# First attention of a transformer kernel: sums of the softmax from a ones column in V, and products on the two 64-row halves of the array, two heads at a time

## The chip, the cores and the metric

The program runs on one core of a Trainium2 chip. One launch computes two blocks of a small transformer. The time is the device time of one launch in microseconds (us). Five engines run their own instruction streams and meet at semaphores: PE (TensorE, products), DVE (VectorE), ACT (ScalarE), POOL (GpSimd) and SP, which issues most of the DMAs.

## The reference, cut to what matters

256 tokens, width 1024, 16 heads of 64. Everything is fp32. The stage that changes is the forgetting attention of the first block:

```python
def forgetting_attention(q, k, v, logf_cum):
    seq = q.shape[1]
    scale = HEAD_DIM ** -0.5
    qf = q.astype(jnp.float32)
    kf = k.astype(jnp.float32)
    outs = []
    for blk in range(seq // Q_BLOCK):
        q0 = blk * Q_BLOCK
        q1 = q0 + Q_BLOCK
        s = jnp.einsum("bqhd,bkhd->bhqk", qf[:, q0:q1], kf[:, :q1]) * scale
        s = s + logf_cum[:, :, q0:q1, None] - logf_cum[:, :, None, :q1]
        mask = (q0 + jnp.arange(Q_BLOCK))[:, None] >= jnp.arange(q1)[None, :]
        s = jnp.where(mask, s, -jnp.inf)
        p = jax.nn.softmax(s, axis=-1).astype(v.dtype)
        outs.append(jnp.einsum("bhqk,bkhd->bqhd", p, v[:, :q1]))
    return jnp.concatenate(outs, axis=1)
...
            o = forgetting_attention(q, k, v, logf_cum).reshape(bsz, seq, D_MODEL)
            x = x + o @ w_o[b_i]
```

`logf_cum` is the running sum of the forget gates' logarithms, one row per head. The term of the query is constant along a softmax row and falls out of it, so the kernel adds only the term of the key. Before it come the projections to K, V and Q, after it the product with `w_o`, then a router and eight experts, then the second block. All of these stay as they are, except for the order of the first of the four `w_o` tiles.

## The kernel before, in words

All order is written out by hand: each engine has one list of instructions, and semaphores join them. PSUM has eight banks. `bank(n)` is use n of banks 0 to 3, taken round robin (`turn`); PE may write a bank again when whoever read its last use has counted up `taken`. `lbank(n)` is use n of banks 4 to 7 (`lend`, `lent_back`) in the same manner. Weights come as tiles of 128 x 2048: SP loads a tile into `ring`, ACT rounds it to `w_hi` (`feed`, L1000), DVE makes the rest `w_lo` (`feed_lo`, L1655), and a product of weights is three products, high by high, high by low and low by high (L2555 to L2557).

The attention works on 32 units. Unit i is head i // 2 and query block i % 2; a unit has k_len = 128 keys for block 0 and 256 for block 1. `attend_step` gives for each unit, on PE: the score product (L2799) of `q_pad` with `kT`, an fp32 product, of which every one stands as two rows (two passes) in the trace; `kT` holds two heads on its 128 rows, so `q_pad` comes in two copies, each with the other head's 64 rows zero. Then, into the same bank, the forget sums in two fp32r products, high part `c_hi` (L2804) and low part `c_lo` (L2805), each by a broadcast column of an identity that picks the head's row; and the causal mask (L2806). DVE takes the negative row maximum (L1948). ACT takes the exponential and its row sum (L1087; the sum is a second instruction). DVE takes the reciprocal of the sum (L1954) and multiplies the probabilities by it (L1955). PE turns the probabilities in blocks of 128 x 128 (L2814), ACT copies them out of PSUM (L1093), and PE multiplies `v_tok`, both heads of a pair wide and stationary, by them (L2826, fp32, two passes). The result has features on the partitions. Scores run ahead: the turn of unit i comes LAG = 3 units after its scores and the product with V two more later. Of each result 64 rows count, and ACT and DVE split them into high and low (L1047, L1051; L1936, L1940), upper and lower half apart, since the next product needs both as its moving part. Three weight tiles of `w_o` are made by DVE inside the stage, after units 5, 10 and 15. Four groups of two products of `w_o` follow (`project`), and the first waits until the last pair of heads is split.

Of the kernel before, what the change touches and what calls it, by code (L numbers as in the profile page):

```python
# [13 lines left out]
P = 128  # L14
# [41 lines left out]
V_LAG = 2  # L56
FIRST_CONSTS = 5
# [3 lines left out]
def build(nc, a):  # L61

    with ExitStack() as ctx:
# [90 lines left out]
        q_pad = [region(4096, DC, T), region(10240, DC, T)]  # L154
        kT = region(6144, DC, T)
        v_tok = region(8192, TT, D)
# [4 lines left out]
        c_hi = act_hi[:, 0, 0:T]  # L161
        c_lo = act_lo[:, 0, 0:T]
# [117 lines left out]
        half_logs = tab(544, 2 * TT * LH)  # L280
        top_i = sb("top_i", [P, TT, 8], U32)
# [74 lines left out]
        def attention_order(units):  # L356

            s, w = {}, {}
            for i in range(units + LAG):
                if i < units:  # L360
                    s[i] = turn(1)
                if i >= LAG:
                    w[i - LAG] = turn(1)
            return s, w

        AT1 = attention_order(2 * NH)
# [133 lines left out]
        A_O1 = lend(8)  # L500
# [123 lines left out]
        heads_done = sem("heads_done")  # L624
        consts = sem("consts")
# [31 lines left out]
        q_padded = sem("q_padded")  # L657
# [207 lines left out]
        def _(pool):  # L865
# [49 lines left out]
            pool.memset(q_pad[0], 0.0)  # L915
            pool.memset(q_pad[1], 0.0).then_inc(q_padded, 1)
            pool.wait_ge(summed, PAIRS)
            pool.memset(c_hi.bitcast(F32), 0.0)
            pool.memset(c_lo.bitcast(F32), 0.0).then_inc(c_padded, 1)
# [40 lines left out]
        def _(eng):  # L960
# [120 lines left out]
            def attend_step(i, order, units, causal, base, sc=sc, pT=pT):  # L1081

                s_use, w_use = order
                if i < units:
                    eng.wait_ge(sc_ready, base + i + 1)
                    k_len = P * (i % 2 + 1) if causal else T
                    give(eng.activation(sc[:, i % 4, 0:k_len], bank(s_use[i])[:, 0:k_len], ACT.Exp,  # L1087
                                        bias=nmax[:, i % 4, :], accum_out=esum[:, i % 4, :]), s_use[i])
                if LAG <= i < units + LAG:
                    j = i - LAG  # L1090
                    k_len = P * (j % 2 + 1) if causal else T
                    eng.wait_ge(done, w_use[j] + 1)
                    give(eng.activation(pT[:, j % pT.shape[1], 0:k_len], bank(w_use[j])[:, 0:k_len], ACT.Copy), w_use[j])  # L1093

            def attend(order, units, causal, base, a_o, h_o, dst_at):

                left = list(range(units // 4))
                for i in range(units + LAG):
                    attend_step(i, order, units, causal, base)
# [2359 lines left out]
```

## Time and profile before

| | us |
|---|---|
| median of three runs | 2083.45 |
| lowest and highest | 2080.48, 2083.79 |
| the profiled execution | 2080.59 |
| its span | 2078.8 |
| from the first score product to the first product of `w_o` | 446.69 to 491.91, that is 45.22 |

The span runs from the first to the last instruction, and 1.8 us lie around it. PE is busy for 96% of it. A matmul's row ends by a model, so the start of the next row tells more than the length of one: where n rows of a kind stand together, the step between starts is (whole length less one row's length) divided by n - 1. Rows named PEld are loads of the stationary part. Times are from the start of the span; a bracket gives the idle time of the engine before the instruction and what ended it.

### The profile page before, as it was taken

How to read it: one execution, taken by the hardware profiler on the slowest of the kernel's cores; microseconds unless marked ns; L12 is line 12 of the kernel's file. 1: busy time of each engine (PE TensorE's matmuls, PEld its weight loads, DVE VectorE, ACT ScalarE, POOL GpSimd, SP SyncE). 2: the span in 40 equal slices, each digit the busy share in tenths (PEclk: the TensorE clock that was granted, in tenths of full speed). 3: DMA queues.
4: the chain of work that ended last, by engine and by line, in shares of the span. 5: the costliest groups of instructions: out<-in, count | busy, mean ns of one | idle time of the engine just before them, and what ended most of it. 6: DMA issues, size and time to landing. Idle time of an engine off the chain costs nothing.

```text
span 2078.8 us, 32665 instructions
## 1 busy us (share of the span) xinstructions
PE 1994.7 (96%) x13049; PEld 1782.3 (86%) x13049; DVE 1510.1 (73%) x1745; ACT 1246.6 (60%) x1477; POOL 38.8 (2%) x69
## 2 busy tenths in 40 slices
PE   8999999989799999999999999899899999999998
PEld 8988899989688888787888888799899998998997
DVE  6966777665688888888888988866656555756554
ACT  5674443555577777777777776746345445775443
POOL 2000000000000000000000000000000000000000
PEclk9999999999899999999999999989999999999999
DMA  8314555532599999989898989635014554424552
GB/s 251 103 44 153 188 182 184 164 120 102 179 359 336 379 340 337 382 326 394 325 394 325 394 323 395 215 99 172 23 41 150 196 184 141 143 99 146 191 186 98
DMA packets 265219, 455.44 MB, mean 219 GB/s; under 512 B 10545, under 2 KB 147226, under 8 KB 265114
## 3 DMA queue, kind: packets, MB, share of 16 engines
q1 hardware_dynamic: 263304, 448.37, 61.6%
q0 software_dynamic: 1424, 5.24, 0.6%
q8 instruction: 78, 1.28, 0.3%
q10 hardware_dynamic: 386, 0.32, 0.0%
q14 instruction: 27, 0.22, 0.0%
HBM read 451.81 MB, written 2.10 MB: 218 GB/s over the span
## 4 chain that ended last, share of the span: by engine, by line
PE 81%; DVE 8%; ACT 5%; issue 3%; DMA 2%; SPq 1%; DVEq 0%; ACTq 0%
PE bank L2555 22%; PE bank L2556 21%; PE bank L2557 21%; PE bank L2743 3%; PE bank L2693 2%; DVE w_lo L1655 2%; DVE w_lo L2069 2%; PE bank L2745 2%; DMA ring<-in_moe_w_up 1%; ACT w_hi L1303 1%; ACT w_hi L1000 1%; PE bank L2959 1%; PE bank L2583 1%; PE bank L2799 1%; PE bank L2826 1%
## 5 line engine op out<-in xcount | busy, mean ns | idle before, releaser
L1655 DVE TENSOR_TENSOR w_lo<-ring,w_hi 128x2048 fp32r<-128x2048 f32 x160 | 365.5, 2292 | 196.7 <-ACT w_hi L1000 196.4
L2555 PE MATMUL bank<-w_hi,a_both 128*128 128x512 f32 (+1 forms) x1040 | 372.5, 358 | 14.8 <-DVE w_lo L2069 11.5
L2555 PE MATMUL bank<-a_both,w_hi 128*128 128x256 f32 x1248 | 360.1, 289 | 10.9 <-DVE a_both L1692 3.9
L2557 PE MATMUL bank<-w_hi,a_both 128*128 128x512 f32 (+1 forms) x1040 | 363.5, 350 | 0.0
L2556 PE MATMUL bank<-w_lo,a_both 128*128 128x512 f32 (+1 forms) x1040 | 363.5, 350 | 0.0
L2069 DVE TENSOR_TENSOR w_lo<-ring,w_hi 128x2048 fp32r<-128x2048 f32 x144 | 327.7, 2290 | 47.8 <-ACT w_hi L1303 47.8
L1000 ACT ACTIVATE w_hi<-ring 128x2048 fp32r<-128x2048 f32 x160 | 304.6, 1908 | 92.7 <-PE bank L2557 86.4
L2556 PE MATMUL bank<-a_both,w_hi 128*128 128x256 f32 x1248 | 355.3, 285 | 0.0
L2557 PE MATMUL bank<-a_both,w_lo 128*128 128x256 f32 x1248 | 355.2, 285 | 0.0
L1303 ACT ACTIVATE w_hi<-ring 128x2048 fp32r<-128x2048 f32 x144 | 276.1, 1919 | 95.5 <-PE bank L2557 84.3
L2069 DVE TENSOR_TENSOR w_lo<-work,w_hi 128x2048 fp32r<-128x2048 f32 x120 | 274.7, 2289 | 21.0 <-ACT w_hi L1303 19.6
L1303 ACT ACTIVATE w_hi<-work 128x2048 fp32r<-128x2048 f32 x120 | 230.5, 1921 | 91.3 <-PE bank L2557 86.4
L2555 PEld LDWEIGHTS bank<-a_both,w_hi 128*128 128x128 f32 x1248 | 241.6, 194 | 15.6 <-issue 9.6
L2556 PEld LDWEIGHTS bank<-a_both,w_hi 128*128 128x128 f32 x1248 | 241.7, 194 | 1.4
L2555 PEld LDWEIGHTS bank<-w_hi,a_both 128*128 128x128 f32 x1040 | 197.3, 190 | 52.6 <-DVE w_lo L2069 25.2
L2557 PEld LDWEIGHTS bank<-a_both,w_lo 128*128 128x128 f32 x1248 | 241.6, 194 | 0.0
L2555 PE MATMUL bank<-w_hi,act_hi 128*128 128x512 f32 x608 | 240.7, 396 | 0.0
L2556 PE MATMUL bank<-w_lo,act_hi 128*128 128x512 f32 x608 | 237.1, 390 | 0.0
L2557 PE MATMUL bank<-w_hi,act_lo 128*128 128x512 f32 x608 | 237.1, 390 | 0.0
L2557 PEld LDWEIGHTS bank<-w_hi,a_both 128*128 128x128 f32 x1040 | 197.2, 190 | 26.4
L2556 PEld LDWEIGHTS bank<-w_lo,a_both 128*128 128x128 f32 x1040 | 197.4, 190 | 23.5
L2555 PEld LDWEIGHTS bank<-w_hi,act_hi 128*128 128x128 f32 x608 | 114.2, 188 | 27.1 <-issue 4.8
(462 smaller groups left out, 2756.1 us busy)
## 6 DMA issues: line engine op xcount, KB each, us to landing
ring<-in_moe_w_up SPq DMA_DIRECT2D x72, 1024.0 KB, 8.2
work<-in_moe_w_gate SPq DMA_DIRECT2D x72, 1024.0 KB, 9.0
ring<-in_moe_w_down SPq DMA_DIRECT2D x56, 1024.0 KB, 6.8
work<-in_moe_w_down SPq DMA_DIRECT2D x32, 1024.0 KB, 7.3
ring<-in_w_up SPq DMA_DIRECT2D x32, 1024.0 KB, 5.5
ring<-in_w_down SPq DMA_DIRECT2D x32, 1024.0 KB, 4.9
ring<-in_moe_w_gate SPq DMA_DIRECT2D x16, 1024.0 KB, 5.1
work<-in_moe_w_up SPq DMA_DIRECT2D x16, 1024.0 KB, 7.5
```

What stands on the lines that cost most here:

```text
L1000: return eng.activation(w_hi[:, slot, :], ring[:, slot, :], ACT.Copy)
L1303: eng.activation(w_hi[:, slot, :], raw_tile(j), ACT.Copy).then_inc(m_hi, 1)
L1655: V.tensor_tensor(w_lo[:, i % SLOTS, :], ring[:, i % SLOTS, :], w_hi[:, i % SLOTS, :].bitcast(F32), ALU.subtract).then_inc(lo_made, 1)
L2069: V.tensor_tensor(w_lo[:, slot, :], raw_tile(j), w_hi[:, slot, :].bitcast(F32), ALU.subtract).then_inc(m_lo, 1)
L2555: PE.matmul(out, left[0], right[0], start=start, stop=False, **kw)
L2556: PE.matmul(out, left[0], right[1], start=False, stop=False, **kw)
L2557: return PE.matmul(out, left[1], right[0], start=False, stop=stop, **kw)
L2583: mm = PE.matmul(bank(n)[:, 0:T], ones[:, :], sq[:, c, :], start=(c == 0), stop=(c == DC - 1))
L2693: mm = PE.matmul(out[:, 0:T], diag[:, i % DIAGS, :], glu[:, c, k:k + T], start=(i == first), stop=(i == DIAG_ENDS[g]))
L2743: PE.matmul(bank(n + i)[:, :].rearrange("p (k t) -> p k t", k=2), w_of[0], a_both[:, :, c, :], start=(c == 0), stop=False, skip_group_chec ...
L2745: mm = PE.matmul(bank(n + i)[:, 0:T], w_of[1], a_hi[:, c, :], start=False, stop=(c == DC - 1), skip_group_check=True)
L2799: mm = PE.matmul(out[:, 0:k_len], q_of(hh)[:, P * j:P * j + P], k_of(hh)[:, 0:k_len], start=True, stop=not causal)
```

## The change

Query, key and cumulative sums:

- `q_pad` becomes `q_sb`, one copy without zeros. The scores of two heads of a pair are two products of 64 rows, head 0 on rows 0 to 63 and head 1 on rows 64 to 127 of the array, into two banks.
- `c_hi` and `c_lo` become one tile `c_two`: rows 0 to 15 hold the high and rows 32 to 47 the low part, and the same again from row 64. `pass_two` is a column pattern with a one in both places, so a single fp32r product of 64 rows adds high and low. ACT and DVE each write one part more, and DVE makes `pass_two` with two small additions.
- V has a 65th column of ones for each head. The row sum is no longer taken by ACT nor applied to the probabilities: the turned probabilities are now stationary and V moves, 65 columns at a time, so the result has tokens on the partitions and the sums in a column. DVE takes the reciprocal for four (head, block) results and multiplies them in one instruction into `o_sb`. PE turns `o_sb` back to features (`turn_heads`), ACT and DVE split the turned bank over all 128 rows.

Order: step m has the two heads of pair m // 2 at query block m % 2. PE's step is scores of m, turns of m - 1, product with V of m - 2, and at odd m from 5 on the turning back of pair (m - 5) // 2. The first `w_o` tile goes by chunks, both banks in turn, each chunk waiting for its pair of heads; the last pair is turned back between chunks 3 and 4. The memory attentions of the second block keep their way, with the parameter for causal calls taken out.

PE, in the middle of the attention, before (units of 256 and 128 keys in turn; bank4 takes the product with V):

```order
L2799 MATMUL bank3<-work 128x256 [waits taken3]
L2804 MATMUL bank3<-act_hi 128x256
L2805 MATMUL bank3<-act_lo,act_hi 128x256
L2806 MATMUL bank3<-act_hi 128x128
L2814 MATMUL bank0<-ident,work 128x128 [waits prob_ready,taken0]
L2826 MATMUL bank4<-work 128x128 [waits taken0]
L2799 MATMUL bank1<-work 128x128 [waits taken1]
L2804 MATMUL bank1<-act_hi 128x128
L2805 MATMUL bank1<-act_lo,act_hi 128x128
L2806 MATMUL bank1<-act_hi 128x128
```

and PE there after the change, one step of 256 keys and the head of the next (L2860 scores, L2863 forget sums, L2865 mask, L2871 turns, L2881 V):

```order
L2860 MATMUL bank3<-work 128x256
L2863 MATMUL bank2<-act_hi,act_lo 128x256
L2863 MATMUL bank3<-act_hi,act_lo 128x256
L2865 MATMUL bank2<-act_hi 128x128
L2865 MATMUL bank3<-act_hi 128x128
L2871 MATMUL bank0<-ident,work 128x128 [waits taken2,taken0]
L2871 MATMUL bank1<-ident,work 128x128 [waits taken3,taken1]
L2881 MATMUL bank4<-work 128x65 [waits taken0]
L2881 MATMUL bank4<-work 128x65
L2881 MATMUL bank4<-work 128x65 [waits taken1]
L2881 MATMUL bank4<-work 128x65
L2860 MATMUL bank2<-work 128x128 [waits taken3,taken2]
```

Scores now use banks 2 and 3 at every step and turned probabilities banks 0 and 1, where before the two kinds took all four in turn.

DVE in the same stretch, before:

```order
L1948 TENSOR_REDUCE small<-bank3 128x1 [waits done]
L1954 RECIPROCAL small<-small 128x1 [waits taken1]
L1955 TENSOR_SCALAR work<-work,small 128x128 [waits vq]
L1948 TENSOR_REDUCE small<-bank1 128x1 [waits done]
L1954 RECIPROCAL small<-small 128x1 [waits taken3]
L1955 TENSOR_SCALAR work<-work,small 128x256 [waits vq]
L1936 TENSOR_TENSOR a_both<-bank4,a_both 64x256 [waits in_hi]
```

and after (L1961 maxima, L1975 and L1976 the division by the sums, L1665 a weight tile, L1940 the split):

```order
L1961 TENSOR_REDUCE small<-bank2 128x1 [waits done]
L1961 TENSOR_REDUCE small<-bank3 128x1 [waits done]
L1975 RECIPROCAL small<-bank6 128x4 [waits heads_done]
L1976 TENSOR_TENSOR work<-bank6,small 128x256 [waits vq]
L1961 TENSOR_REDUCE small<-bank2 128x1 [waits done]
L1961 TENSOR_REDUCE small<-bank3 128x1 [waits done]
L1665 TENSOR_TENSOR w_lo<-ring,w_hi 128x2048 [waits hi_made]
L1940 TENSOR_TENSOR a_both<-bank5,a_both 128x256 [waits in_hi]
```

The reciprocal and the scaling of each unit are gone from between the maxima. The weight tile still stands between two maxima.

The core of the diff, in the order forget sums and bank uses, ACT's loop, DVE's query part, division and loop, PE's loop and first `w_o` tile:

```diff
-        q_pad = [region(4096, DC, T), region(10240, DC, T)]
+        q_sb = region(4064, DC, T)
-        v_tok = region(8192, TT, D)
+        v_tok = region(8160, TT * NH, HD + 1).rearrange("p (j h) e -> p j h e", j=TT)
-        c_hi = act_hi[:, 0, 0:T]
-        c_lo = act_lo[:, 0, 0:T]
+        c_two = act_hi[:, 0, 0:T]
+        pass_two = act_lo[:, 0, 0:NH]
...
-        AT1 = attention_order(2 * NH)
+        AT1 = {}, {}
+        for m in range(NH + 1):
+            for i in range(2 * m, 2 * m + 2):
+                if m < NH:
+                    AT1[0][i] = turn(1)
+            for i in range(2 * m - 2, 2 * m):
+                if m:
+                    AT1[1][i] = turn(1)
...
+            def attend_tokens(order):
+                for m in range(NH + 1):
+                    k_len = P * (m % 2 + 1)
+                    for i in range(2 * m, 2 * m + 2):
+                        if m < NH:
+                            eng.wait_ge(sc_ready, i + 1)
+                            give(eng.activation(sc[:, i % 4, 0:k_len], bank(s_use[i])[:, 0:k_len], ACT.Exp, bias=nmax[:, i % 4, :]), s_use[i])
+                    if m % 2 == 0 and m > TURN_LAG:
+                        turned_heads_hi((m - TURN_LAG - 1) // 2)
+                    k_len = P * ((m - 1) % 2 + 1)
+                    for i in range(2 * m - 2, 2 * m):
+                        if m:
+                            eng.wait_ge(done, w_use[i] + 1)
+                            give(eng.activation(pT[:, i % 4, 0:k_len], bank(w_use[i])[:, 0:k_len], ACT.Copy), w_use[i])
...
-                V.scalar_tensor_tensor(q_pad[0][0:64, i, :], bank(n)[0:64, 0:T], HD ** -0.5, rstd[0:64, :], ALU.mult, ALU.mult)
-                give(V.scalar_tensor_tensor(q_pad[1][64:P, i, :], bank(n)[64:P, 0:T], HD ** -0.5, rstd[64:P, :], ALU.mult, ALU.mult), n)
+                give(V.scalar_tensor_tensor(q_sb[:, i, :], bank(n)[:, 0:T], HD ** -0.5, rstd[:, :], ALU.mult, ALU.mult), n)
...
+            def heads_by_sums(c):
+                n = A_O1 + 2 * c
+                eng.wait_ge(heads_done, c + 1)
+                out = lbank(n)[:, 0:4 * (HD + 1)].rearrange("p (u e) -> p u e", u=4)
+                link(V.reciprocal(head_rec[:, c % 2, :], out[:, :, HD]))
+                give_lent(V.tensor_tensor(o_sb[:, c % 2, :].rearrange("p (u e) -> p u e", u=4), out[:, :, 0:HD],
+                                          head_rec[:, c % 2, :].rearrange("p (u o) -> p u o", o=1).to_broadcast([P, 4, HD]), ALU.mult), n)
...
+                for m in range(NH):
+                    for i in range(2 * m, 2 * m + 2):
+                        score_max(i, order, P * (m % 2 + 1))
+                    if m in (2, 5, 7):
+                        feed_lo(min(T_Q + (m + 1) // 3 + SLOTS + (m == 7), T_MOE - 1))
+                    if m % 2 == 0 and m >= 4:
+                        heads_by_sums(m // 2 - 2)
+                    if m % 2 == 1 and m >= TURN_LAG + 2:
+                        heads_back((m - TURN_LAG - 2) // 2)
...
+                        outs = [open_bank(s_use[2 * m + r]) for r in range(2)]
+                        for r, at in HALVES:
+                            PE.matmul(outs[r][:, 0:k_len], q_sb[at, c, P * j:P * j + P], kT[at, c, 0:k_len], start=True, stop=False)
+                        for r, at in HALVES:
+                            one = pass_two[at, 2 * c + r:2 * c + r + 1].to_broadcast([CK, P])
+                            PE.matmul(outs[r][:, 0:k_len], one, c_two[at, 0:k_len], start=False, stop=False)
+                        for r, at in HALVES:
+                            PE.matmul(outs[r][:, P * j:P * j + P], pass_on, causal_mask, start=False, stop=True).then_inc(done, 1)
...
+                                mm = PE.matmul(out[:, at:at + HD + 1], pT[:, t % 4, P * b:P * b + P], v_tok[:, b, 2 * c + r, :], start=(b == 0), stop=(b == j))
...
-            for t in range(4):
-                if t == 0:
-                    got_lent(eng, A_O1 + 6)
-                    got_lent(eng, A_O1 + 7)
+            outs = [open_bank(U_WO), open_bank(U_WO + 1)]
+            for c in range(DC):
+                if c == DC - 4:
+                    turn_heads(DC - 1)
+                got_lent(eng, A_O1 + 2 * c + 1)
+                for i in range(2):
+                    mm = product(outs[i][:, 0:T], [v[:, c, P * i:P * i + P] for v in w], a_part(c), c == 0, c == DC - 1)
+                    if c == DC - 1:
+                        mm.then_inc(done, 1)
+            for t in range(1, 4):
                 project(T_WO + t, U_WO + 2 * t)
```

## Rows read from the trace of the kernel before

**Rows 1.** The page: busy time and share of each engine; the group of weight tiles' low parts.

```profile
PE 1994.7 (96%) x13049; PEld 1782.3 (86%) x13049; DVE 1510.1 (73%) x1745; ACT 1246.6 (60%) x1477; POOL 38.8 (2%) x69
...
L1655 DVE TENSOR_TENSOR w_lo<-ring,w_hi 128x2048 fp32r<-128x2048 f32 x160 | 365.5, 2292 | 196.7 <-ACT w_hi L1000 196.4
```

**Rows 2.** Stretches: length, busy PE, PEld, DVE, ACT, POOL (instructions), granted clock, DMA.

```profile
446.70:472.20 25.50, 20.88 (x162) 19.49 (x163) 20.77 (x61) 15.60 (x58) 0.00 (x0) 1.00 0.29 90
472.20:486.00 13.80, 13.80 (x118) 13.47 (x116) 11.85 (x43) 10.66 (x45) 0.00 (x0) 1.00 0.17 65
```

**Rows 3.** The chain that ended last, in order of time: start, length, what.

```profile
474.53 0.43 PE bank L2799 x2
...
485.91 0.43 PE bank L2799 x2
```

**Rows 4.** Timeline of PE, late in the attention: start, length, engine, line, operation.

```profile
485.30 0.61 PE L2826 MATMUL bank<-work 128*128 128x128 f32 x4
...
486.30 0.28 PE L2805 MATMUL bank<-act_lo,act_hi 128*128 128x256 f32 x1
486.41 0.22 PE L2806 MATMUL bank<-act_hi 128*128 128x128 f32 x1
```

**Rows 5.** Timeline of all engines at the start of the attention.

```profile
446.05 0.43 DVE L1919 SCALAR_TENSOR_TENSOR work<-bank,rstd 64x256 f32<-64x256 f32 x1
...
446.69 0.46 PE L2799 MATMUL bank<-work 128*128 128x128 f32 x2 [1.10 <-DVE work L1919]
...
447.15 0.28 PE L2806 MATMUL bank<-act_hi 128*128 128x128 f32 x1
...
447.47 0.29 DVE L1948 TENSOR_REDUCE small<-bank 128x1 f32<-128x128 f32 x1 [0.99 <-PE bank L2806]
...
449.13 0.37 ACT L1087 ACTIVATE work<-bank,small 128x128 f32<-128x128 f32 x1
```

**Rows 6.** Timeline of ACT, one of three places where a weight tile on DVE delays it.

```profile
462.95 0.47 ACT L1087 ACTIVATE work<-bank,small 128x256 f32<-128x256 f32 x1 [2.12 <-DVE small L1948]
```

**Rows 7.** Groups of DVE and ACT by line and shape: count, busy us, mean ns, idle before.

```profile
L1948 DVE TENSOR_REDUCE small<-bank 128x1 f32<-128x256 f32 x32 | 13.5, 422 | 6.9 <-PE bank L2799 3.4 <-PE bank L2806 3.2
...
L1087 ACT ACTIVATE work<-bank,small 128x256 f32<-128x256 f32 x32 | 15.1, 473 | 32.1 <-DVE small L1948 32.0
...
L1093 ACT ACTIVATE work<-bank 128x256 f32<-128x256 f32 x24 | 9.0, 377 | 0.4 <-PE bank L2814 0.3
```

**Rows 8.** Timeline of PE in the second block: products of 64 rows among full ones.

```profile
1826.87 0.61 PE L2826 MATMUL bank<-work,mem_v 128*128 128x128 f32 x4
1827.41 0.71 PE L3345 MATMUL bank<-work 64*128 64x256 f32 x4
...
1828.17 0.59 PE L3345 MATMUL bank<-work 64*128 64x256 f32 x2
1828.61 0.38 PE L3346 MATMUL bank<-work 64*128 64x128 f32 x2
1828.92 0.38 PE L2555 MATMUL bank<-w_hi,a_both 128*128 128x256 f32 x1
```

**Rows 9.** Timeline of PE in the second block: fp32 products that move 64 columns, then 128.

```profile
1509.58 0.39 PE L3222 MATMUL bank<-work 128*128 128x64 f32 x2
...
1510.03 0.39 PE L3222 MATMUL bank<-work 128*128 128x64 f32 x2
1510.25 1.56 PE L3228 MATMUL bank<-work 128*128 128x128 f32 x12
```

**Rows 10.** Timeline of PE at the end of the attention: the first product of `w_o`.

```profile
491.91 0.35 PE L2555 MATMUL bank<-a_both,w_hi 128*128 128x256 f32 x1 [1.80 <-issue]
```

**Rows 11.** PE in the second block: two stretches (clock after the busy time), one timeline row.

```profile
1496.00:1498.00 2.00, 1.89 (x32) 0.87 0.00 0
1498.00:1500.00 2.00, 1.39 (x7) 0.50 0.03 8
...
1501.20 2.88 PE L3228 MATMUL bank<-work 128*128 128x128 f32 x12
```

More of the change, by code:

```diff
@@ L1079, in ffn, with attend_step @@
                         feed(tile_of[g - 1][-1] + SLOTS)
-            def attend_step(i, order, units, causal, base, sc=sc, pT=pT):
+            def attend_step(i, order, units, base, sc=sc, pT=pT):
                 s_use, w_use = order
@@ L1090, in attend_step, with turned_heads_hi @@
                     j = i - LAG
-                    k_len = P * (j % 2 + 1) if causal else T
                     eng.wait_ge(done, w_use[j] + 1)
[L1093 to L1099, printed above, removed]
-                    if 9 <= i < units and i % 4 == 1:
-                        split_upper(a_o + left[0], h_o + left[0], dst_at + left[0])
-                    if 9 <= i < units and i % 4 == 3:
-                        c = left.pop(0)
-                        split_lower(a_o + c, dst_at + c)
-                for c in left:
-                    split_pair(a_o + c, h_o + c, dst_at + c)
+                    give(eng.activation(pT[:, j % pT.shape[1], 0:T], bank(w_use[j])[:, 0:T], ACT.Copy), w_use[j])
+            def turned_heads_hi(c):
+                eng.wait_ge(heads_turned, c + 1)
+                eng.activation(a_hi[:, c, :], lbank(A_O1 + 2 * c + 1)[:, 0:T], ACT.Copy).then_inc(in_hi, 1)
+            def attend_tokens(order):
+                s_use, w_use = order
+                for m in range(NH + 1):
[11 more added lines that the diff above has]
+                            give(eng.activation(pT[:, i % 4, 0:k_len], bank(w_use[i])[:, 0:k_len], ACT.Copy), w_use[i])
+                for c in range((NH - TURN_LAG - 1) // 2 + 1, DC):
+                    turned_heads_hi(c)
             def scaled_hi(u, gain):
@@ new lines, in heads_back, with attend_tokens @@
+            def heads_back(c):
+                heads_lo(A_O1 + 2 * c + 1, I_WO, c)
+            def attend_tokens(order):
+                for m in range(NH):
[7 more added lines that the diff above has]
+                        heads_back((m - TURN_LAG - 2) // 2)
+                for c in range(DC - 2, DC):
+                    heads_by_sums(c)
+                    heads_back(c - 1)
+                heads_back(DC - 1)
@@ L2824, in attend_step, with turn_heads @@
                     got(eng, w_use[t])
-                    for b in range(blocks):
+                    for b in range(TT):
                         mm = PE.matmul(out[:, at:at + P], v_of(hh, b), pT[:, t % pT.shape[1], P * b:P * b + P],
-                                       start=(b == 0), stop=(b == blocks - 1))
+                                       start=(b == 0), stop=(b == TT - 1))
                     if t % 4 == 3:
                         mm.then_inc(heads_done, 1)
-            def attend(order, units, causal, base, a_o, q_of, k_of, v_of):
-                for i in range(units + LAG + V_LAG):
-                    attend_step(i, order, units, causal, base, a_o, q_of, k_of, v_of)
+            def turn_heads(c):
+                got_lent(eng, A_O1 + 2 * c)
+                out = open_lent(A_O1 + 2 * c + 1)
+                for j in range(TT):
+                    mm = PE.transpose(out[:, P * j:P * j + P], o_sb[:, c % 2, P * j:P * j + P], ident[:, :])
+                mm.then_inc(heads_turned, 1)
```

142 lines of the change are left out of this document (69 added, 73 removed).

## Prediction, made before the changed kernel had run

> **What bounds the kernel now.** The page comes first: PE is busy for 96% of the span [rows 1], so a change is worth what it takes from PE's path or from a wait of PE. I then cut the attention, 446.69 to 491.91 us, into stretches. Late in it, from 472.2 to 486.0, PE is busy without a gap, DVE for 11.85 and ACT for 10.66 of 13.80 us: PE bounds. Before, from 446.7 to 472.2, PE is busy for 20.88 of 25.50 us [rows 2], and the reasons are the start and three weight tiles of 2.29 us on DVE [rows 1], each of which keeps the maxima and so ACT waiting (2.12 us in one place [rows 6]). After the last scores PE works off the tail until 491.91 [rows 10]. The chain of waits shows the steady pace: the 256-key score products of two units ten units apart stand at 474.53 and 485.91 [rows 3], 11.38 us for five heads, 2.28 each or 4.55 for a pair.
>
> **Prices of PE.** All of these are starts, not lengths. A full fp32 pass with 128 columns comes every (0.61 - 0.27) / 3 = 0.113 us, and the fp32r forget product of 256 columns is followed after 0.11 by the mask [rows 4]. By these a pair of heads before costs: scores 4 x (0.22 + 0.113) = 1.33 (two passes of 256 columns take from 1828.17 to 1828.61 in [rows 8]), forget sums 8 x 0.115 = 0.92, mask 4 x 0.113 = 0.45, turns 6 and V 12 passes x 0.113 = 2.03: 4.73, against 4.55 measured, so the list holds to 4%.
>
> **Part by part, on PE, for a pair.**
> *Scores on halves.* The nearest rows are in the second block, where L3345 (256 columns) and L3346 (128) work on 64 rows, three heads in turn on halves 0, 1, 0 [rows 8]. The first four L3345 stand together, so the second head's passes began before the first head's narrower ones: the halves do overlap. Two heads took 1828.17 - 1827.41 = 0.76 us, where one alone took 0.75 to the next full product. So I take 0.50 for 256 keys and 0.25 for 128, against 0.88 and 0.45 if the halves ran one after the other.
> *Changing between 64 and 128 rows.* The last full pass begins at 1826.87 + 0.61 - 0.27 = 1827.21 and should be through at 1827.32; the half one starts at 1827.41. On the way back the last pass begins at 1828.72, is through at 1828.83, and the full one starts at 1828.92. So each change costs 0.09 us, and there are two in a step, 0.36 in a pair. The Trainium skill, "TensorEngine Tiling (Array Packing)", Key Properties, speaks against the change here: switching the tiling mode drains the engine. The rows agree that it costs something, and I go by their 0.09.
> *Forget sums.* Eight products become two concurrent pairs, 0.12 each, 0.24. No row shows fp32r on 64 rows; without overlap they cost 0.46.
> *Mask, turns.* The same numbers, 4 and 6, 1.13; turning back adds 2, 0.23.
> *V.* Still 12 passes, now with 65 columns instead of 128. Rows 9 have the price of that: from 1509.58 to 1510.03 four passes that move 64 columns, 0.112 each, and the same at 128 columns, (1.56 - 0.27) / 11 = 0.117. Half the columns save nothing, since each pass has its own load of 128 stationary columns. So 12 x 0.113 = 1.36. The Trainium skill, "TensorE: Matmul & The Clock Gate", Back-to-back issue gap, would have the step follow the moving columns down to about 60; by that V would cost about half. The rows say no.
> The sum for a pair is 0.75 + 0.36 + 0.24 + 1.13 + 0.23 + 1.36 = 4.07. By steps: odd m (256 keys: scores 0.50, sums 0.12, changes 0.18, mask 0.23, two turns 0.23, eight passes of V 0.90, turning back 0.23) 2.38; even m 1.68.
>
> **The loop that takes PE's place.** Scores always use banks 2 and 3, so the scores of step m + 1 wait for both exponentials of step m. At 256 keys: scores, sums and change 0.71 to the first mask product; 0.32 from there to DVE's start (447.15 to 447.47 [rows 5]); one maximum's step 0.34 and the second maximum 0.42; ACT 0.04 later for 0.47 [rows 7]; 0.05 back to PE: 2.35. At 128 keys with 0.29 and 0.37 [rows 5]: 0.46 + 0.32 + 0.20 + 0.29 + 0.04 + 0.37 + 0.05 = 1.73. A pair makes 4.08. PE and this loop are equal to within the reading, which leaves no slack, so I take 4.15 for a pair, 1.75 for a lone even step. DVE's own load is 1.4 of maxima, 0.2 + 0.42 for the division, 0.42 for the split, about 2.4; ACT's 2 x (0.47 + 0.37) of exponentials, 2 x 0.38 + 2 x 0.27 of copies and 0.38 for the split, 3.4: both below 4.15, and the copies end about when the next exponential is due.
>
> **Start, tiles, tail.**
> *Start.* The query part on DVE is one instruction of 0.43 instead of two, so the first scores come 0.43 earlier, at 446.26 [rows 5]. Steps 0 and 1 have free banks. The first exponential comes 2.44 after the first scores, as before (446.69 to 449.13); four exponentials, 2 x 0.27 and 2 x 0.38 apart, end 1.4 later, and step 2 starts at 3.9. Steps 2 to 14 are six pairs and one even step: 6 x 4.15 + 1.75 = 26.65.
> *Weight tiles.* They stand after the maxima of steps 2, 5 and 7. A tile of 2.29 begins 1.25 (even) or 1.75 (odd) into the step; the next maximum is due 0.75 to 1.0 into the next step. So it is late by about 0.8, 0.9 and, with a split behind it, 1.25: 2.9.
> *Tail.* Step 15 takes 2.38. Then come four turns and V of step 14, 0.9; V of step 15 follows the copies, 0.95; turning back 0.23; then `w_o` starts: 4.5 in all. The rest of the last pairs' splitting lies beside the products of chunks 0 to 6, 0.72 each; before it stood open.
> The sum is 3.9 + 26.65 + 2.9 + 4.5 = 37.95 from first score to first `w_o` product, against 45.22. With the 0.43 the gain is 7.7 us. What follows has no fixed point in time: the first expert tiles released by the first bank of `w_o` come 2.9 later in that tile but earlier absolutely, and experts start 50 us later. ACT's and DVE's extra parts of `c_two`, some 1.2 us about 390 us, fall where DVE and ACT wait for PE and PE has work; uncovered they would cost at most 1.2. POOL's shorter fills cost nothing.
>
> On the profiled execution's own time 2080.6 - 7.7 = 2072.9 would follow. It lay 2.9 below the median of 2083.45, inside the runs' own spread; the forecast is for the median, 2083.45 - 7.7 = **2075.8 us**.
>
> **Rivals.**
> *The loop is slower than its parts.* If each step's chain loses 0.3 us (maxima behind a division, an exponential behind the copies), a pair takes 4.7 and the gain is 7.7 - 6.5 x 0.55 = 4.1: 2079.4. For it: two engines stand at their limit with nothing ahead in the banks. Against: DVE and ACT have 1 us a pair free. 18%.
> *The halves do not overlap*, because each head's passes reach the queue in pairs or fp32r behaves otherwise: scores cost 0.58 and sums 0.22 more a pair, 0.80 x 8 = 6.4, gain 1.3: 2082.2. This is also the case in which the change doesn't do what it says. Rows 8 speak against it. 9%.
> *Clock, the slower side.* The new stage streams fewer columns in each microsecond and has a wait of 2 us at its start. In the second block the granted clock fell to 0.50 (1.2 GHz) at 1498, after PE had run small products of 64 rows and 64 columns; twelve passes then took 2.88 instead of 1.56 us [rows 9, 11]. At that level a pair's 4.07 of PE would become about 8, 3.9 more. The gain is eaten after two pairs, and the kernel is slower by over 0.2% from three on, some 24 us at half clock. With three pairs it gives 2083.45 - 7.7 + 11.7 = 2087.5. Against it: before, the clock stayed at 1.00 with PE busy for 82% [rows 2]. 7%.
> *Better.* By the skill's rule on short products V would take 0.7 less a pair, but the loop of 4.08 stays; only 0.1 a pair and some of the tail are left, about 1.5 in all: 2074.3. 5%.
>
> **How the numbers follow.** The forecast holds 61%, with 2 us either way for the pace of a pair (0.15 x 7), the tail and the runs' spread. About 0.2%, 4.2 us, is what a measurement can tell from no change. Faster by more takes nearly all of the forecast's share (0.58), the better case and half of the slow loop: 0.72. Within 0.2%: the rest of these and most of the halves' case, 0.20. Slower: the clock and a little, 0.08. The range reaches from 2071.5, below the better case by the spread, to 2083.0, past the halves' case, and leaves out the clock's.
>
> **What would show each step.** In the changed profile: the two heads' score passes starting within 0.1 us of each other and a 256-key step's scores through in 0.5; V's passes 0.11 apart; steps of 2.4 and 1.75; before each score product a wait near zero that ends with an exponential; three waits of about 1 us behind weight tiles; first `w_o` product at 484.2; granted clock 1.00. It is wrong if score steps come more than 4.5 a pair apart, if halves run in turn, or if the clock row of the stage falls.

## Result and the profile after: slower, and half the clock for nearly the whole stage

| | median us | from | to | runs |
|---|---|---|---|---|
| before | 2081.86 | 2079.68 | 2083.79 | 5 |
| after | 2096.07 | 2093.14 | 2100.55 | 5 |

The ratio is 1.0072 with a 95% interval of 1.0058 to 1.0086: slower by 14 us, where 7.7 less were forecast. The profiled execution of after took 2098.95 us with a span of 2097.2. The page of after, where [rows 1] stood: busy time, the clock in 40 slices (in tenths of full speed), and the group of weight tiles.

```profile
PE 2018.1 (96%) x13033; PEld 1799.6 (86%) x13033; DVE 1493.8 (71%) x1684; ACT 1239.9 (59%) x1438; POOL 34.9 (2%) x67
...
PEclk9999999976899999999999999989999999999999
...
L1665 DVE TENSOR_TENSOR w_lo<-ring,w_hi 128x2048 fp32r<-128x2048 f32 x160 | 365.1, 2289 | 200.3 <-ACT w_hi L1001 200.1
```

PE has 16 instructions fewer and is busy 23 us longer. DVE and ACT became lighter, as forecast. So PE's instructions became slower, and the stretches say where (columns as in [rows 2]: length, busy PE, PEld, DVE, ACT, POOL, granted clock, DMA). A granted clock of 1.00 is 2.4 GHz, one of 0.50 is 1.2 GHz:

```profile
446.00:450.00 4.00, 2.18 (x18) 1.63 (x17) 1.67 (x5) 3.78 (x5) 0.00 (x0) 1.00 0.00 0
450.00:454.00 4.00, 3.57 (x20) 3.06 (x20) 1.74 (x3) 2.28 (x9) 0.00 (x0) 0.56 0.01 2
454.00:458.00 4.00, 4.00 (x19) 3.38 (x18) 1.71 (x3) 1.17 (x4) 0.00 (x0) 0.50 0.44 137
...
446.75:506.68 59.93, 58.35 (x287) 50.47 (x287) 22.46 (x56) 23.24 (x72) 0.00 (x0) 0.53 0.17 53
472.20:486.00 13.80, 13.80 (x68) 11.61 (x68) 5.14 (x15) 4.06 (x14) 0.00 (x0) 0.50 0.24 77
```

The stage from the first scores to the first `w_o` product takes 59.93 us instead of 45.22: 14.7 more, close to the difference of the medians (14.2). The two profiled executions lie 18.4 apart. The granted clock also falls to 0.50 in some ten short places outside the stage, in before as in after; summed over stretches of 2 us these make some 68 us in before and 77 in this execution of after, which at half clock is worth roughly the rest. Within 4 us of the stage's start the clock falls to 0.50, and there it stays until after the stage, with PE busy without a gap. In 472.20 to 486.00 PE got through 68 instructions, where before it got through 118 in the same time [rows 2]. The timeline of PE at the start and in the steady part (L2860 scores, L2871 turns, L2881 V, L2848 turning back, L2578 `w_o`):

```profile
446.75 0.46 PE L2860 MATMUL bank<-work 64*128 64x128 f32 x3 [0.67 <-DVE work L1933]
...
449.93 0.56 PE L2871 MATMUL bank<-ident,work 128*128 128x128 f32 x2 [1.15 <-ACT work L1107]
450.92 0.80 PE L2860 MATMUL bank<-work 64*128 64x128 f32 x4 [0.43 <-ACT work L1107]
...
465.56 0.80 PE L2860 MATMUL bank<-work 64*128 64x128 f32 x4
...
470.92 1.81 PE L2881 MATMUL bank<-work 128*128 128x65 f32 x8
472.53 0.63 PE L2848 MATMUL bank<-ident,work 128*128 128x128 f32 x2
473.09 0.80 PE L2860 MATMUL bank<-work 64*128 64x128 f32 x4
...
506.68 0.56 PE L2578 MATMUL bank<-a_both,w_hi 128*128 128x256 f32 x1
```

Three waits in the first steps (0.67, 1.15, 0.43) end on the query part and on exponentials. After them PE waits for nobody: from 465.56 to 473.09 a pair of heads takes 7.53 us, against 4.55 before [rows 3]. Eight passes of V take from 470.92 to 472.53, 0.20 each, against 0.113 in [rows 4]. At 1.2 GHz PE alone is the bound, and no term of the loop of maxima and exponentials that was forecast can be read. The first question is therefore what the changed stage costs at a full clock; the second, why the clock fell and didn't come back.

### The profile page after: what moved, and what is told of

It reads as the page before. It is cut to its first block, busy times and chain, and to the rows that moved or that the text cites. A ratio compares the mean times of both kernels' runs of the same rounds, so it can differ in the third digit from the quotient of the medians.

```text
span 2097.2 us, 32554 instructions
## 1 busy us (share of the span) xinstructions
PE 2018.1 (96%) x13033; PEld 1799.6 (86%) x13033; DVE 1493.8 (71%) x1684; ACT 1239.9 (59%) x1438; POOL 34.9 (2%) x67
## 4 chain that ended last, share of the span: by engine, by line
PE 84%; DVE 6%; ACT 4%; issue 3%; DMA 1%; SPq 1%; DVEq 0%; ACTq 0%
PE bank L2578 22%; PE bank L2579 21%; PE bank L2580 21%; PE bank L2766 3%; PE bank L2716 2%; PE bank L2768 2%; DVE w_lo L2092 2%; DVE w_lo L1665 1%; ACT w_hi L1313 1%; DMA ring<-in_moe_w_up 1%; ACT w_hi L1001 1%; PE bank L3014 1%; PE bank L2881 1%; PE bank L2606 1%; PE bank L2687 1%
## 5 line engine op out<-in xcount | busy, mean ns | idle before, releaser
L1665 DVE TENSOR_TENSOR w_lo<-ring,w_hi 128x2048 fp32r<-128x2048 f32 x160 | 365.1, 2289 | 200.3 <-ACT w_hi L1001 200.1
L2578 PE MATMUL bank<-w_hi,a_both 128*128 128x512 f32 (+1 forms) x1040 | 373.3, 359 | 15.2 <-DVE w_lo L2092 12.0
L2578 PE MATMUL bank<-a_both,w_hi 128*128 128x256 f32 x1248 | 359.8, 288 | 8.0 <-DVE a_both L1702 3.9
L2578 PEld LDWEIGHTS bank<-a_both,w_hi 128*128 128x128 f32 x1248 | 241.0, 193 | 12.4 <-issue 7.2
L2578 PEld LDWEIGHTS bank<-w_hi,a_both 128*128 128x128 f32 x1040 | 197.9, 190 | 53.0 <-DVE w_lo L2092 25.5
L2578 PE MATMUL bank<-w_hi,act_hi 128*128 128x512 f32 x608 | 241.1, 397 | 0.0
L2578 PEld LDWEIGHTS bank<-w_hi,act_hi 128*128 128x128 f32 x608 | 114.7, 189 | 26.9 <-issue 4.6
```

The lines of the kernel that those rows point to most:

```text
L1665: V.tensor_tensor(w_lo[:, i % SLOTS, :], ring[:, i % SLOTS, :], w_hi[:, i % SLOTS, :].bitcast(F32), ALU.subtract).then_inc(lo_made, 1)
L2578: PE.matmul(out, left[0], right[0], start=start, stop=False, **kw)
```

## Experiments

"Stage" is the time from the first scores to the first `w_o` product in the profiled execution.

### The clock alone: work for PE in the thin start

```diff
+                    if m == 2:
+                        filler(4)
...
+                    if m == 1:
+                        filler(10)
```

`filler(n)` is n fp32r products of 128 rows and 256 columns into a bank that nobody reads. They stand where PE waits for the first exponentials, and they hold nothing up: step 2 starts 4.16 us after the first scores with them, 4.17 without.

> The changed kernel with 14 idle-filling products added on PE (fp32r, 128 rows, 256 columns, into a PSUM bank whose content nobody reads): ten between the scores of step 1 and the first turn, four before the scores of step 2, which is where PE waited 1.15 and 0.43 us for ACT and where the granted clock fell from 1.00 to 0.50. Theory G (the waits at the start bring the clock down, and the stage as such would hold it): clock 1.00 through the stage, first w_o product near 485 us, total near 2075. Theory D (the stage's own stream of short products lets the clock fall, whatever the start): clock 0.50 some us later than in the changed kernel, total 2090 to 2096.

2074.89 us, against 2085.41 for the kernel before beside it. The granted clock is 1.00 throughout the stage, and the stage takes 39.44 us. The stretch of the stage, then PE, DVE and ACT in steady state (L2868 scores, L2871 forget sums, L2873 mask, L2881 turns, L2891 V):

```profile
446.89:486.33 39.44, 35.79 (x301) 30.88 (x301) 22.06 (x55) 23.00 (x72) 0.00 (x0) 1.00 0.25 81
```

```profile
475.43 0.46 PE L2868 MATMUL bank<-work 64*128 64x128 f32 x3
475.65 0.30 PE L2871 MATMUL bank<-act_hi,act_lo 64*128 64x128 f32 x1
...
475.68 0.30 PE L2871 MATMUL bank<-act_hi,act_lo 64*128 64x128 f32 x1
...
475.92 0.44 PE L2873 MATMUL bank<-act_hi 128*128 128x128 f32 x2
...
477.38 0.67 PE L2868 MATMUL bank<-work 64*128 64x256 f32 x3 [0.17 <-ACT work L1107]
...
478.13 0.44 PE L2873 MATMUL bank<-act_hi 128*128 128x128 f32 x2
...
478.65 1.00 PE L2891 MATMUL bank<-work 128*128 128x65 f32 x8
479.49 0.39 PE L2848 MATMUL bank<-ident,work 128*128 128x128 f32 x2
479.94 0.46 PE L2868 MATMUL bank<-work 64*128 64x128 f32 x3
```

```profile
478.49 0.76 DVE L1961 TENSOR_REDUCE small<-bank 128x1 f32<-128x256 f32 x2 [1.17 <-PE bank L2873]
```

```profile
478.95 0.84 ACT L1107 ACTIVATE work<-bank,small 128x256 f32<-128x256 f32 x2 [0.89 <-DVE small L1961]
```

So 14 added products, which compute nothing, save some 20 us: the clock is the whole of the miss, and at a full clock the changed stage is 5.8 us shorter than the old one. What it takes is read below.

Timed in five rounds:

> The kernel with the filled start once more, now timed in five rounds. If filling the start removes the fall and not by luck: granted clock 0.98 in every execution, median 2075 to 2077, ratio to before 0.995 to 0.998. If the fall depends on when the stage begins: some executions near 2095.

Median 2074.65 us (2070.27 to 2093.47, 12 runs) against 2084.63 (17 runs), ratio 0.9962 [0.9942, 0.9982]. Of the twelve, one stood at 2093.47 us with a mean clock of 0.974, the others at 0.980 to 0.987. That is where a stage that loses its clock would stand, but that execution was not profiled, so it is an inference.

### Which half of the change leaves the clock down

V moved 128 columns instead of 65 (the next head's columns, read and not used):

```diff
-  PE.matmul(out[:, at:at + HD + 1], pT[...], v_tok[:, b, 2 * c + r, :], ...)
+  v_at = (HD + 1) * (NH * b + 2 * c + r)
+  PE.matmul(out[:, at:at + 128], pT[...], v_flat[:, v_at:v_at + 128], ...)
```

> The changed kernel with the product with V moving 128 columns instead of 65 (63 further columns of V, whose results fall on places that the next product rewrites or nobody reads). At either clock the loads of the stationary part set V's pace, 0.113 or 0.217 us a pass, so the wider stream costs nothing by itself. Theory D-V (V's half-empty stream is what keeps the clock down): clock 1.00 for most of the stage, total 2075 to 2082. Theory G or D-rows (the start, or the 64-row products): clock stays at 0.50, total 2094 to 2097.

2079.81 us (before 2085.41), stage 40.34. The same thin start, and the clock falls as it did in after, but it comes back 3.4 us later:

```profile
448.00:452.00 4.00, 2.42 (x19) 1.73 (x16) 1.10 (x4) 3.00 (x8) 0.00 (x0) 0.98 0.01 2
452.00:456.00 4.00, 4.00 (x22) 3.25 (x22) 3.10 (x4) 1.61 (x6) 0.00 (x0) 0.60 0.11 21
456.00:460.00 4.00, 3.78 (x33) 3.16 (x33) 1.41 (x6) 1.90 (x8) 0.00 (x0) 1.00 0.79 245
```

Timed:

> The changed kernel with one edit, V moved 128 columns instead of 65 (64 of them read and not used, the next head's columns), timed. Theory, that the 64-row products hold a clock but do not lift a fallen one, and the wider V does: 2076 to 2081 us, 0.995 to 0.999 of the kernel before, which is 15 us or more under the changed kernel at 2096. Rival, that its one profiled execution was a lucky one: a median between 2085 and 2096 us.

Median 2078.81 us (2071.15 to 2084.58, 10 runs) against 2082.29 (29 runs): 0.9985 [0.9971, 0.9999]. One edit that adds columns takes 17 us off the changed kernel. In its profiled execution the clock fell at about 453.3 and was back 3.4 us later, as in the first one.

Scores and forget sums on all 128 rows, the queries padded with zeros as before, V left at 65 (of the edit the scores; the forget sums likewise):

```diff
-  PE.matmul(outs[r][:, 0:k_len], q_sb[at, c, ...], kT[at, c, 0:k_len], ...)
+  PE.matmul(outs[r][:, 0:k_len], q_pad[r][:, c, ...], kT[:, c, 0:k_len], ...)
```

> The changed kernel with scores and forget sums as products of 128 rows again (two zero-padded copies of the queries, the upper half of c_two left zero), all else as changed: ones column, 65 moving columns of V, order by steps. By rows at full clock scores cost 0.58 and sums 0.2 us a pair more. Theory D-rows (the 64-row products keep the clock down): clock 1.00, pair 4.85 us, first w_o product near 490, total near 2081. Theory D-V or G: clock 0.50, a pair then costs 7.1 + 1.6 = 8.7, total 2105 or more.

2080.18 us (before 2085.41), stage 42.31, clock 1.00 throughout the stage. PE at a start nearly as thin, and a pair in steady state (L2863 scores):

```profile
446.00:450.00 4.00, 2.40 (x16) 2.19 (x16) 1.94 (x6) 3.47 (x4) 0.00 (x0) 1.00 0.00 0
450.00:454.00 4.00, 3.16 (x21) 2.75 (x22) 1.87 (x4) 2.60 (x10) 0.00 (x0) 1.00 0.01 2
```

```profile
474.63 1.10 PE L2863 MATMUL bank<-work 128*128 128x256 f32 x4 [0.17 <-ACT work L1110]
...
479.62 1.10 PE L2863 MATMUL bank<-work 128*128 128x256 f32 x4 [0.17 <-ACT work L1110]
```

A pair takes 4.99 us against 4.51: the two halves are worth 0.48 a pair at a full clock, as long as they don't take the clock with them. Since the clock didn't fall here, this run can't say whether 128 rows bring a fallen one back; a pause further down does.

Fillers and wide V together, for the question whether V's columns cost anything when the clock is up anyway:

> Both of the first two edits together: filled start and 128 moving columns of V. If start and V's stream work together (neither alone is enough): clock 1.00 and total near 2075 here, 2090 and more in both single ones. If one alone is enough, this equals it within 2 us. If the clock still falls here, the 64-row products or the turns are the reason.

2079.34 us (before 2085.41), stage 39.45 against 39.44 with the fillers alone. The second half of V's columns costs the stage 0.01 us over 96 passes. On PE it isn't quite free: eight passes of 128 columns take 0.89 us where eight of 65 take 0.84 (474.95 to 475.84 here, 478.65 to 479.49 with the fillers alone), but in this stage PE then waits that much less. The whole is 4.5 us longer than in the first experiment. The other places where the clock falls account for it: outside the stage it stood at 0.50 for some 78 us here and some 68 there, which costs about 5. Two executions of one kernel differ in the same way: with the fillers alone, one of 2074.89 us had 68 us at 0.50 and one of 2081.80 had 86, while their stages took 39.44 and 39.38. In five rounds:

> The fillers and the 128 moved columns of V together, timed against the kernel before. Theory, that the fillers alone leave a kernel that once in a while loses its clock for the whole stage (one execution of twelve stood at 2093.5 us, at the time of the kernel without fillers), and that the wider V lifts it within a few us: median 2073 to 2078 us, the ratio 0.993 to 0.998, and no execution above 2088. Rival, that the execution at 2093.5 us came from something else: the same median and again one or two executions of a dozen near 2093.

Median 2077.81 us (2070.28 to 2080.98, 12 runs) against 2082.29: 0.9974 [0.9961, 0.9986]. None of the twelve stands near 2093. Against one of twelve without the wide V that proves little.

### Lifting and lowering the clock on purpose

A dense burst in mid stage, without fillers at the start: 30 of the filler's products before the scores of step 8.

> The changed kernel (thin start, clock expected at 0.50 from about 451 us) with 30 back-to-back products of 128 rows and 256 columns put before the scores of step 8, into a PSUM bank whose content nobody reads. They take some 6.5 us at half clock. Theory H (two stable states: the stage holds a full clock but cannot raise a fallen one): the clock returns to 1.00 in or right after the burst and stays to the end of the stage, steps 8 to 15 at 4.5 us a pair, first w_o product near 497, total near 2087. Theory D (the stage's stream is too thin for full clock at all, and the filled start was luck): the clock falls again within some steps, first w_o product at 509 or later, total near 2100.

2085.58 us (before 2084.63), stage 52.46:

```profile
466.00:470.00 4.00, 4.00 (x24) 3.49 (x22) 1.59 (x5) 1.45 (x5) 0.00 (x0) 0.50 0.54 159
470.00:474.00 4.00, 3.80 (x20) 2.95 (x16) 2.85 (x3) 1.18 (x4) 0.00 (x0) 0.50 0.27 103
474.00:478.00 4.00, 3.51 (x16) 3.51 (x17) 0.44 (x2) 0.00 (x0) 0.00 (x0) 0.50 0.63 213
478.00:482.00 4.00, 3.83 (x34) 3.52 (x33) 1.00 (x4) 0.87 (x4) 0.00 (x0) 0.96 0.13 49
482.00:486.00 4.00, 3.94 (x36) 3.43 (x36) 1.75 (x7) 2.12 (x9) 0.00 (x0) 1.00 0.02 4
```

The burst runs from 474.49 to about 480; behind it the same steps that had gone at 0.50 go at 1.00 to the end. So the changed stage runs at either clock, and in this run each of the two lasted as long as the stage's own steps ran by themselves.

The other way round: a pause of PE in a stage that had its clock. With the fillers at the start, two dependent additions of DVE over 1936 columns (4.37 us, read by nobody) stand ahead of the maxima of step 8. PE stands idle for 5.5 us because of them:

```diff
+                    if m == 8:
+                        for k in range(2):
+                            link(V.tensor_tensor(idle_to, idle_from, idle_from, ALU.add))
```

> The kernel with the filled start (clock 1.00 through the stage, total 2075) and two extra DVE instructions of about 2 us each, whose output nobody reads, before the maxima of step 8: PE then waits some 3 to 4 us once in the middle of the stage. Theory H: the clock falls to 0.50 there and stays until w_o, so steps 8 to 15 cost 7.3 instead of 4.5 us a pair, first w_o product near 500, total near 2090. If only the start of the stage is special: the clock stays or comes back by itself, the cost is the pause, 3 to 4 us, total 2079.

> As the run with the pause, and V moving 128 columns instead of 65. Theory H with V's stream as what keeps a fallen clock down: the clock falls at the pause and comes back within about 5 us, first w_o product near 492, total near 2082 and some 8 us less than with 65 columns. If V's stream is not the reason, both are equal.

With V at 65 columns: 2090.75 us, stage 53.55. The clock fell in the pause, at about 469.5, and stood at 0.50 up to about 496.9. With V at 128: 2081.84 us, stage 46.2, and the clock was back 6.8 us after its fall:

```profile
466.00:470.00 4.00, 1.21 (x10) 1.01 (x10) 3.97 (x4) 0.00 (x0) 0.00 (x0) 1.00 0.56 164
470.00:474.00 4.00, 1.36 (x6) 0.90 (x6) 2.52 (x5) 1.45 (x5) 0.00 (x0) 0.63 0.33 129
474.00:478.00 4.00, 4.00 (x23) 3.59 (x21) 1.09 (x3) 1.18 (x4) 0.00 (x0) 0.52 0.01 4
478.00:482.00 4.00, 3.88 (x32) 3.27 (x31) 2.09 (x7) 2.42 (x9) 0.00 (x0) 1.00 0.00 0
```

Then one pause for three kernels (three additions over 1192 columns, 4.26 us; PE idle for 5.2 to 5.6): the kernel before, the changed kernel with full rows and V at 65, the changed kernel with fillers.

> The kernel before, whose scores, forget sums and V products all move 128 or 256 columns over 128 rows, with three dependent additions of VectorE over 1192 columns (their output is read by nobody) put ahead of the row maxima of the ninth unit of two, so that PE stands for about 4 us in mid stage. Theory, that a fallen clock is lifted again by the products of this kernel but not by the short and half-height ones of the changed kernel: the granted clock falls to 0.50 after the pause for 4 to 10 us and is 1.00 again until the output projection; the stage goes from 45.2 to 51 to 54 us (4 of pause, 2 to 5 of half clock). Rival, that any pause inside attention leaves half a clock up to the output projection: 0.50 from the pause on, and the stage comes out at 60 us or more. Second rival, that a pause of this length does not touch the clock: stage 49 to 49.5 us, clock 1.00.

> The changed kernel with scores and forget sums on all 128 rows (no fillers, V still 65 columns), and the same pause of three dependent additions over 1192 columns ahead of the maxima of step 8, whose output nobody reads. Theory A, that products of all 128 rows lift a fallen clock as V of 128 columns does, each edit being enough alone: the granted clock falls to 0.50 after the pause for 4 to 12 us and is 1.00 again before the output projection; stage 42.3 + 4 + 2 to 5 = 48 to 52 us. Theory B, that only V's 128 moved columns lift it, and full rows merely kept the thin start busier: 0.50 from the pause to the output projection, stage 56 to 60 us. Theory C, that full rows keep the clock up through the pause: 1.00 throughout, stage 46 to 47 us.

> The changed kernel with the fourteen fillers at the start and the pause of the same three additions over 1192 columns ahead of the maxima of step 8. Theory, that the short V products and the 64-row products together cannot lift a fallen clock: 0.50 from the end of the pause for all of the remaining steps, 1.00 from the output projection on, stage 52 to 56 us (39.4 + 4 of pause + 9 to 12 of half clock). Rival, that the fall which the longer additions of the earlier pause brought about was chance: 0.50 for at most 8 us, stage 46 to 48 us.

| kernel, pause in each | stage | without pause | at 0.50 |
|---|---|---|---|
| before | 51.87 | 45.22 | some 7 us, then 1.00 |
| full rows, V 65 | 48.09 | 42.31 | some 7 us, then 1.00 |
| halves, V 65, fillers | 56.30 | 39.4 | to the end of the stage |

The stretches of the full-rows kernel, and those of the one with halves:

```profile
470.00:474.00 4.00, 0.00 (x0) 0.00 (x0) 3.90 (x5) 0.00 (x0) 0.00 (x0) 0.73 0.79 262
474.00:478.00 4.00, 3.22 (x12) 2.88 (x12) 1.29 (x5) 1.59 (x6) 0.00 (x0) 0.50 0.00 0
478.00:482.00 4.00, 3.84 (x30) 3.68 (x29) 1.49 (x6) 2.47 (x9) 0.00 (x0) 0.92 0.00 0
```

```profile
470.00:474.00 4.00, 1.06 (x6) 0.91 (x6) 2.79 (x6) 1.44 (x5) 0.00 (x0) 0.65 0.42 163
474.00:478.00 4.00, 4.00 (x24) 3.36 (x20) 1.08 (x3) 1.17 (x4) 0.00 (x0) 0.50 0.00 0
...
494.00:498.00 4.00, 4.00 (x20) 3.36 (x19) 1.41 (x6) 1.56 (x6) 0.00 (x0) 0.50 0.01 2
```

Theory A of the full-rows run stands, on one execution. Each of the two edits alone, 128 rows or 128 columns of V, was enough to bring the clock back; only the changed kernel's own mix of 64-row products and 65 columns left it down. The turns (some 1.6 of the 7.53 us of a pair at 0.50) stayed as they are in all runs of the changed kernel, so what part they have in it was not tested. The mix isn't quite unable to: with the first pause the clock rose at 496.9, in the middle of step 15, after some 27 us at 0.50. In after, in the burst run and in the last one it didn't rise for as long as the mix ran by itself.

### What bounds the stage once the clock is up

The fillers and V of 128, and the row maximum of an odd step over its first 128 keys only (softmax allows any shift from which the exponentials don't overflow):

```diff
-                        score_max(i, order, P * (m % 2 + 1))
+                        score_max(i, order, P)
```

> The changed kernel with the fourteen fillers of the first experiment, V moved 128 columns, and the row maximum of an odd step read over the first 128 keys only instead of 256. (Any shift gives the same softmax; the row sums come out of the ones column as before.) If the loop scores, maximum, exponential, next scores sets the pace of the stage at full clock, the odd step loses what a reduction of 128 fewer columns saves, about 0.27 us, on four of its reductions per two pairs: the step of two heads goes from 4.51 to about 4.2 us and the stage from 39.45 to 37.0 to 38.0 us, and the whole kernel goes to 2072 to 2076 us. If PE's own work or the wait for weight tiles sets the pace, nothing moves: stage 39.2 to 39.7 us. If shorter waits of VectorE let PE run closer, the granted clock stays 1.00 either way; a clock below 0.90 anywhere in the stage would speak against the reading that V's columns hold it up.

Median 2075.0 us (2069.91 to 2078.77, 11 runs) against 2082.29: 0.9969 [0.9958, 0.9980]. Stage 38.47, 1.0 less than with the full maximum; 1.4 to 2.4 were expected. The scores (L2872) and V (L2896):

```profile
471.76 0.67 PE L2872 MATMUL bank<-work 64*128 64x256 f32 x3
...
473.02 1.06 PE L2896 MATMUL bank<-work 128*128 128x128 f32 x8
...
474.23 0.49 PE L2872 MATMUL bank<-work 64*128 64x128 f32 x4
...
476.17 0.67 PE L2872 MATMUL bank<-work 64*128 64x256 f32 x3
```

An odd step takes 2.47 instead of 2.56, an even one 1.94 as before (its maximum was 128 wide already). So the loop through DVE and ACT bounded the odd step too, but PE's own work stands 0.1 behind it: the odd step's next scores at 474.23 wait for nobody. This version and the one with fillers alone are the fastest run here, and the intervals don't tell them apart.

## Why the prediction was wrong, point by point

**The step that failed is the clock.** The rival "Clock, the slower side" had the mechanism, the sign and the bound (slower from three pairs on, some 24 us at half clock), and 7%. What spoke against it was "before, the clock stayed at 1.00 with PE busy for 82% [rows 2]". That argued from the busy share of products of 128 rows and 128 to 256 columns to a stage of other products. The rows that bore on it were named beside it: after small products of 64 rows and 64 columns the clock was down [rows 11], and it stood there while twelve passes ran [rows 11]. The price for three pairs was mis-sized as well: it took for granted that a fallen clock comes back soon, which in after it didn't within the stage. The price of one pair was near: 7.53 us at half clock, where about 8 were forecast. Measured, 59.93 - 39.44 = 20.5 us are lost, less the 5.8 that the change gains at a full clock: 14.7. The Trainium skill, "TensorE: Matmul & The Clock Gate", Part 1, lets the clock follow how busy PE has lately been and has it return once PE is busy. The trace of after disagrees for this mix of products: PE was busy for 4.00 of 4.00 us in stretch after stretch at 0.50.

**At a full clock the sum held to 1.5 us.** The stage was put at 37.95 and measured at 39.44, so the gain there is 5.8 and not 7.3. The whole kernel comes nearer than that deserves: by the ratio, 0.9962 x 2083.45 = 2075.5, for 2075.8 forecast, but the interval of that ratio reaches from 3.8 to 12 us of gain, and the stage with its earlier start accounts for 6.2 of them, so the closeness is luck. Term by term, from the run with fillers:

- *Start:* the first scores come 23.96 us after the first query products (422.93 to 446.89), 24.37 before (422.32 to 446.69): 0.41 of the 0.43 is there. In after it can't be seen in absolute time (446.75 against 446.69), because that execution ran 0.48 late long before the changed part. Step 2 at 4.16, forecast 3.9.
- *Halves:* they overlap, also with fp32r. A step of 128 keys comes to its sums after 0.22 and to its mask after 0.49 (forecast 0.25 and 0.46), and the two heads' sums start 0.03 apart. The 9% rival is out.
- *V:* 0.105 a pass at 65 columns, (479.49 - 478.65) / 8, and 0.113 at 128, (473.92 - 473.02) / 8 in the run with the short maximum. Half the columns save less than 0.01 a pass and nothing of the stage, nearly as the rows had said.
- *Pair:* 4.51 instead of 4.15: 2.56 and 1.95 for 2.35 and 1.73. This is the "loop slower" rival at two thirds of its size. PE's path to the mask is 0.03 longer, DVE starts 0.36 after it (forecast 0.32), and the next scores start 0.15 after the exponentials end (478.95 + 0.84 = 479.79, to 479.94), not 0.05. That last step is the largest, some 0.2 a pair, and the 0.05 had no row behind it. The change to 64 rows isn't its reason: in the full-rows run, without any, scores start 0.15 after the exponentials too (476.53 + 0.84 = 477.37, to 477.52). The trace of the kernel before has the price: an exponential runs from 451.14 for 0.47, to 451.61, and the scores that wait for it start at 451.75, 0.14 later:

```profile
451.75 0.70 PE L2799 MATMUL bank<-work 128*128 128x256 f32 x2 [0.43 <-ACT work L1087]
```

  PE's own share, 2.38 forecast for the odd step, is 2.47 at most.
- *Weight tiles:* three waits of 0.67, 0.74 and 1.07 us. What they add to the pace is less, since PE waits a little in other steps too: steps 2 to 14 take 30.83 us (451.05 to 481.88), six pairs of 4.51 and one step of 1.95 make 29.0, so 1.8 are left for the tiles; forecast 2.9.
- *Tail:* from the scores of step 15 (481.88) to `w_o` 4.45; forecast 4.5. The four parts, 4.16 + 29.0 + 1.8 + 4.45, are the 39.4 of the stage.

The range was too narrow on one side for the same reason: it left out the clock's case, whose price is the length of the stage and not a few pairs.

## What to carry to other kernels

A change that makes TensorE's products smaller (fewer rows, fewer moving columns) should be priced at both clocks, and the places where PE starts thinly or pauses in that stage read as places where the clock may fall: ask whether the products behind them have been seen to bring it back. Columns that a pass moves for nothing can be nearly free where, as here, each pass has its own load of 128 stationary columns, and may be worth their keep for the clock alone. The sign that the clock is the cause is plain: PE busy without a gap, fewer instructions in the same time, every other engine idle more.

## What the runs showed of the hardware

- One and the same sequence of products ran at either clock for a long time: at 1.00 over 39 us once it was up, at 0.50 over 56 us once it was down. PE was busy for 3.77 of 4.00 us in the first (478 to 482 with fillers) and for 4.00 of 4.00 in the second.
- The clock came back behind wider or taller products, where PE was no busier: 128 moving columns of V (after 3.4 us at 0.50 in the start, 7 us after its fall in a pause), 128 rows of scores and sums (7 us after its fall in a pause), in a burst of 30 products of 128 rows and 256 columns, or with `w_o`. The last of these, in after:

```profile
502.00:506.00 4.00, 4.00 (x22) 4.00 (x21) 1.03 (x3) 1.42 (x5) 0.00 (x0) 0.50 0.00 0
506.00:510.00 4.00, 4.00 (x26) 4.00 (x26) 1.03 (x3) 0.38 (x1) 0.00 (x0) 0.69 0.02 4
510.00:514.00 4.00, 4.00 (x36) 4.00 (x35) 1.05 (x3) 0.60 (x2) 0.54 (x2) 1.00 0.00 0
```

- A pause of PE brought the clock down in all five runs that had one, four kernels; PE was idle in it for 5.49, 5.44, 5.60, 5.21 and 5.37 us, though the additions took 4.26 or 4.37. The kernel before pays 51.87 - 45.22 = 6.65 us for it, the changed one with fillers 56.30 - 39.4 = 16.9.
- The exponential's end was followed by the start of the scores that wait for it after 0.14 to 0.15 us, with products of 64 rows and of 128.
- Left open: why the clock fell in the start of after and held in that of the full-rows kernel. From the first scores on PE was busy for 2.59 of 4.00 us in after and for 2.96 of 4.00 there, so the starts are not quite the same. Open too is what makes the clock fall in the other places of the program, which is where most of the spread between executions of one kernel seems to lie.
